# Experts ranked by load, with 64-token and 128-token experts in turn, in a mixture-of-experts stage

## The chip, the core and the metric

The kernel runs on one core of a Trainium2 chip. The core has TensorE (PE in the profile; its weight loads are PEld), VectorE (DVE), ScalarE (ACT), GpSimd (POOL) and SyncE (SP), which here only issues transfers, and 16 DMA engines. Each engine runs its own program in order; they wait for each other through semaphores. The metric is the device time of one execution in microseconds (us).

## What is computed

One layer of a diffusion backbone over 256 latent tokens of width 1024 (256 context tokens feed the first half of the layer). The first half is a token mixer (input projection, spatial gating, a gated delta rule, output projection). The second half is a mixture of experts, and that is where the change lies: 16 experts, of which each token takes 2, both from one group of four.

```python
def routed_moe(h, w_router, b_router, w1, w3, w2):
    scores = jax.nn.sigmoid(h @ w_router)
    sel = scores + b_router
    grp_score = jnp.sum(lax.top_k(sel.reshape(-1, N_GROUPS, EXPERTS_PER_GROUP), TOP_K)[0], axis=-1)
    best = jnp.argmax(grp_score, axis=-1)
    in_group = (jnp.arange(N_EXPERTS)[None, :] // EXPERTS_PER_GROUP) == best[:, None]
    _, idx = lax.top_k(jnp.where(in_group, sel, -jnp.inf), TOP_K)
    wts = jnp.take_along_axis(scores, idx, axis=-1)
    wts = wts / jnp.sum(wts, axis=-1, keepdims=True)
    ...
    for e in range(N_EXPERTS):
        y_e = (jax.nn.silu(h @ w1[e]) * (h @ w3[e])) @ w2[e]
        y = y + combine[:, e:e + 1] * y_e
    return y
```

`w1` and `w3` are 1024x512 and `w2` is 512x1024 for each expert, in float32: 6 MB an expert, 100.7 MB in all. 256 tokens x 2 choices are 512 rows of work, 32 an expert on average.

## The kernel before

All is written out by hand, with an order of its own for each engine. The expert stage begins at about 636 us.

**Routing and gather.** VectorE works out the two choices of each token (`chosen`); TensorE counts them, so that `counted` has each expert's number of rows and the first of them, and each of the 512 rows has a place in a list sorted by expert. TensorE gathers the tokens into that order by multiplying with a selection matrix (`pick`). ScalarE and VectorE copy the result to `hT`, split in a high part and a rest: every matmul of the stage is done as hi*hi, hi*lo and lo*hi in the type fp32r. `gather_copy` and `gather_low` are those copies; `h2_lo` is the rest of the tokens.

**An expert.** For each expert, in the order 0 to 15, GpSimd copies a window of 128 columns of `hT` that begins at the expert's first row (`take_window`; expert 0 reads `hT` itself). TensorE multiplies it with `w1` and `w3` (`up_half`, m = 0 and 1; 24 matmuls of 512 columns each), ScalarE takes the silu, VectorE the product (`act_product`), TensorE transposes it (`turn_act`, 4 transposes), ScalarE and VectorE split it (`act_high`, `act_low`), and TensorE multiplies with `w2` (`down_half`, twice 12 matmuls). ScalarE copies the result to `y_out` (`y_copy`) and GpSimd stores it with an indirect DMA, which skips the rows of the window that are not the expert's; the numbers for that come from `store_rows`. The last expert is stored by SP, all 128 rows, behind the 512 others (`LISTED` to `FIRST_TURN`). `place_rows`, on VectorE behind expert 1, works out where each token finds its two rows in the end. An expert of over 128 rows would go through `expert_turn`, which does not run here.

**The weights.** `STREAM` is the order of the 96 units of weights, 128x2048 floats (1 MB) each: the four up units of expert q, then the two down units of expert q-1. SP loads unit n into slot n % 5 (`SLOTS_AHEAD`) when unit n-5 is split. ScalarE casts a unit to `e_hi` (`expert_high`) and VectorE subtracts that from it to `e_lo` (`expert_low`); there are four buffers of each, so that the splits run up to four units ahead of TensorE. The semaphores are `landed`, `hi_ready`, `unit_split` and, for a unit that TensorE is through with, `unit_used`. In the profile the units are `raw`, and `e_hi` and `e_lo` are `w_hi` and `w_lo`.

**The constants.** GpSimd builds masks and counting rows (`order_mask`, `slot_iota`, `slot_row`) at the start of the program. It takes no part in the program between the last scan and the sum of squares `x_stat`.

## Time and profile before

| | us |
|---|---|
| three runs | 932.27, 930.23, 938.56; median 932.27 |
| the profiled execution, its own time | 937.08 |
| its span | 935.4 |
| PE busy | 818.2 (87%) |
| DVE busy | 625.3 (67%) |
| ACT busy | 516.1 (55%) |
| POOL busy | 224.9 (24%) |
| TensorE clock granted, mean | 0.963 |

The span is the time from the first to the last instruction of the profiled execution; its own time has in addition what lies around the instructions. The busy shares are means over stages of different kinds: up to 636 us the mixer, the routing and the gather, then the experts up to about 913 us, then the sum over each token's two rows and the output. In the rows further down, x12 is a count, "idle before" is the time an engine stood still ahead of an instruction, and the arrow names what ended it. The granted clock is 1.00 for 2.4 GHz and 0.50 for 1.2 GHz. A matmul's duration in a row includes its latency; matmuls overlap, so the distance between two starts tells the pace.

### The profile page before, as it was taken

The numbers are of one execution on the slowest core, as the hardware profiler recorded it, in microseconds if no ns is written. First come the engines' busy times: TensorE is split into PE (matmuls) and PEld (weight loads), VectorE is DVE, ScalarE is ACT, GpSimd is POOL, SyncE is SP. The second block draws the span as 40 slices with busy tenths as digits, with TensorE's granted clock in tenths as the row PEclk, the third lists the DMA queues.
The fourth block names the chain that finished last, engine by engine and source line by source line (L and its number), as shares of the span: only waits on it lengthen the run. The fifth ranks groups of instructions, "written<-read, shape, count | busy, mean of one in ns | idle before, by whom it ended". The sixth has DMA issues, their size and how long they took to land. (4 is left out here: it accounts for less than half of the span.)

```text
span 935.4 us, 15876 instructions
## 1 busy us (share of the span) xinstructions
PE 818.2 (87%) x6374; PEld 694.7 (74%) x6374; DVE 625.3 (67%) x804; ACT 516.1 (55%) x814; POOL 224.9 (24%) x336
## 2 busy tenths in 40 slices
PE   4998987999789997798769789949999999999990
PEld 2677875899669885698749788737888888888870
DVE  1596765458643585545455447678998998999965
ACT  3575742457414564236542344467777787777751
POOL 3114061124301243112410110016222322321112
PEclk9999999999989999999889999959999999999995
DMA  9977468345862358536687348807999999999944
GB/s 311 283 241 190 123 162 211 80 108 147 175 187 78 105 152 161 174 80 227 174 211 207 91 158 263 307 18 265 342 364 385 383 380 384 388 371 374 380 144 156
DMA packets 220052, 209.00 MB, mean 223 GB/s; under 512 B 51100, under 2 KB 156229, under 8 KB 219337
## 3 DMA queue, kind: packets, MB, share of 16 engines
q1 hardware_dynamic: 217241, 203.80, 69.5%
q0 software_dynamic: 2736, 4.15, 1.4%
q8 instruction: 52, 0.85, 0.4%
q14 instruction: 23, 0.19, 0.1%
HBM read 190.64 MB, written 23.10 MB: 229 GB/s over the span
## 5 line engine op out<-in xcount | busy, mean ns | idle before, releaser
L2061 DVE TENSOR_TENSOR w_lo<-raw,w_hi 128x2048 fp32r<-128x2048 f32 x96 | 233.3, 2450 | 24.3 <-ACT w_hi L1496 23.2
L2282 PE MATMUL bank<-hT,half_hi 128*128 128x256 f32 (+1 forms) x1024 | 231.1, 321 | 12.1 <-DVE half_lo L1616 5.9
L1496 ACT CAST w_hi<-raw 128x2048 fp32r<-128x2048 f32 x96 | 183.2, 1912 | 41.1 <-PE bank L2282 38.5
L2282 PEld LDWEIGHTS bank<-hT,half_hi 128*128 128x128 f32 x1024 | 169.5, 195 | 28.6 <-issue 8.0
L2282 PE MATMUL bank<-hT,half_lo 128*128 128x256 f32 (+1 forms) x512 | 160.8, 314 | 0.0
L2282 PE MATMUL bank<-w_hi,window 128*128 128x512 f32 x480 | 156.7, 397 | 0.0
L1616 DVE TENSOR_TENSOR half_lo<-half_raw,half_hi 128x1024 fp32r<-128x1024 f32 x88 | 108.8, 1237 | 55.9 <-ACT half_hi L1056 55.4
L2282 PE MATMUL bank<-lane 64*64 64x64 f32 (+2 forms) x2096 | 100.2, 233 | 21.7 <-issue 10.6
L2282 PEld LDWEIGHTS bank<-lane 64*64 64x64 f32 (+2 forms) x2096 | 91.5, 145 | 32.1 <-issue 17.4
L1056 ACT CAST half_hi<-half_raw 128x1024 fp32r<-128x1024 f32 x88 | 92.2, 1049 | 25.1 <-DMA half_raw<-in_w_out_dram 6.7
L2282 PEld LDWEIGHTS bank<-w_hi,window 128*128 128x128 f32 x480 | 90.3, 188 | 20.5
L2282 PEld LDWEIGHTS bank<-hT,half_lo 128*128 128x128 f32 x512 | 99.3, 194 | 5.5
L2282 PE MATMUL bank<-w_lo,window 128*128 128x512 f32 x240 | 94.7, 394 | 0.0
L1712 DVE SCALAR_TENSOR_TENSOR chan<-bank,conv_col,chan 128x508 f32<-128x508 f32 (+3 forms) x96 | 63.2, 658 | 8.1 <-ACT chan L1125 5.5
L967 POOL CAST window<-hT 128x2048 fp32r x15 | 39.7, 2652 | 113.7 <-PE bank L2282 90.0
L882 POOL TENSOR_TENSOR lane<-v_nat,gates 128x256 f32<-128x256 f32 x32 | 25.1, 788 | 142.1 <-DVE lane L1796 120.3
L2282 PEld LDWEIGHTS bank<-w_lo,window 128*128 128x128 f32 x240 | 45.2, 188 | 10.0
L2282 PE MATMUL bank<-w_hi,act_hi 128*128 128x512 f32 x128 | 50.6, 395 | 1.5 <-DVE act_lo L2214 1.5
L997 POOL DMA_INDIRECT expert_rows<-y_out,store_int x15 | 26.7, 1782 | 99.7 <-ACT y_out L1534 99.7
L2282 PE MATMUL bank<-w_hi,act_lo 128*128 128x512 f32 x128 | 50.5, 395 | 0.0
L2282 PE MATMUL bank<-w_lo,act_hi 128*128 128x512 f32 x128 | 50.4, 394 | 0.0
L1133 ACT ACTIVATE tanh_buf<-chan 128x512 f32<-128x512 f32 (+1 forms) x24 | 13.4, 559 | 40.3 <-DVE chan L1712 40.2
(321 smaller groups left out, 1269.2 us busy)
## 6 DMA issues: line engine op xcount, KB each, us to landing
raw<-in_w_e_dram SPq DMA_DIRECT2D x96, 1024.0 KB, 8.8
half_raw<-in_w_in_dram SPq DMA_DIRECT2D x64, 512.0 KB, 5.0
half_raw<-in_w_ada_dram SPq DMA_DIRECT2D x32, 512.0 KB, 4.8
raw<-in_w_ada_dram SPq DMA_DIRECT2D x8, 1024.0 KB, 11.4
dense<-staged SPq DMA_DIRECT2D x32, 128.0 KB, 4.5
half_raw<-in_w_proj_a_dram SPq DMA_DIRECT2D x8, 512.0 KB, 5.3
half_raw<-in_w_proj_b_dram SPq DMA_DIRECT2D x8, 512.0 KB, 4.1
half_raw<-in_w_out_dram SPq DMA_DIRECT2D x8, 512.0 KB, 8.3
```

The source lines that it names most:

```text
L882: last = pool.tensor_tensor(v_beta[pos % 2][:, :, d, :], v_nat[i % 2][:, :, t, :], gates[:, BETA, t, 2 * i:2 * i + 2, d:d + 1].to_broadcas ...
L967: pool.tensor_copy(window[q % 2][:, :, :, :], hT[:, :, :, bass.ds(at, P)].bitcast(F32)) .then_inc(s["window_ready"], 1)
L997: pool.indirect_dma_start(out=y_dram[0:LISTED, :], out_offset=to, in_=y_out[q % 2][:, :], in_offset=None, bounds_check=LISTED - 1, oob_is_ ...
L1056: act.copy(half_hi[m % HBUF][:, :], half_raw[n % HRING][:, :]).then_inc(s["half_high"], 1)
L1133: act.activation(tanh_buf[n % 2][:, 0:w], chan[n % 3][:, 0:w], ACT.Tanh, scale=0.5)\
L1496: act.copy(e_hi[n % WBUF][:, :], slots[n % SLOTS_AHEAD][:, :]).then_inc(s["hi_ready"], 1)
L1616: dve.tensor_tensor(half_lo[m % HBUF][:, :], half_raw[n % HRING][:, :], half_hi[m % HBUF][:, :].bitcast(F32), ALU.subtract).then_inc(s["ha ...
L1712: ins = dve.scalar_tensor_tensor(out=y[:, :, a:b], in0=ps[:, :, a + o:b + o], scalar=conv_col[:, CONV_KIND[n // 2], 2 * j + n % 2, tap:tap ...
L2061: dve.tensor_tensor(e_lo[n % WBUF][:, :], slots[n % SLOTS_AHEAD][:, :], e_hi[n % WBUF][:, :].bitcast(F32), ALU.subtract)\
L2282: return nc.tensor.matmul(dst, lhsT, rhs, start=start, stop=stop)
```

## The change

Experts 0 and 1 stay as they are. The other 14 are ranked by their number of rows when the counts are there, and the stream takes them in an order of ranks, wide and narrow in turn: places 2, 4, 6, 8, 10, 12 and 15 are narrow, 64 tokens, and hold the seven least loaded experts; places 3, 5, 7, 9, 11, 13 and 14 are wide, 128 tokens, and hold the seven most loaded. The eighth most loaded of 512 rows has at most 64. A number (`rank_at`) says which rank stands at which place.

A narrow expert's weights are not split. TensorE reads the f32 unit from its slot, in two column halves of the array: 64 output rows are one half of the columns of a unit, the other 64 the other half. So the expert takes 32 f32 matmuls of 256 columns up, 2 transposes and 8 of 512 down, in place of 48, 4 and 24. ScalarE and VectorE cast and split 54 units in place of 96. The slot of a narrow unit comes free with `unit_used`, not with `unit_split`. The two down units of a narrow expert are waited for together and used in alternation, so both are released by its last matmuls. The window of a narrow expert is the sum of both parts of `hT`, 64 columns. Its result is 128x512 and its store has half the bytes a row.

SP reads the number of the next expert from `order_int` and forms the addresses of the weights from it. VectorE ranks (`rank_loads`) ahead of the first copy of the gather, and orders counts and firsts (`order_experts`) behind the third split. `place_rows` has three operations more, since the last expert in the stream is now any of 14. The constants of GpSimd are built later, and there are more of them.

```diff
-FIRST_TURN = LISTED + 128
+FIRST_TURN = LISTED + 64
...
+WIDE, NARROW = P, P // 2
+FIXED = 2
+RANKED = EXPERTS - FIXED
+WIDTH = [WIDE, WIDE] + 6 * [NARROW, WIDE] + [WIDE, NARROW]
...
+        SPLIT_UNITS = [n for n, (_, q, _) in enumerate(STREAM) if WIDTH[q] == WIDE]
...
+            expert = list(range(FIXED))
             for n, (v, q, half_) in enumerate(STREAM):
-                if n >= SLOTS_AHEAD:
-                    sp.wait_ge(s["unit_split"], n - SLOTS_AHEAD + 1)
...
+                if n == UP_FIRST[FIXED]:
+                    sp.wait_ge(s["routing_ready"], 2)
+                if q == len(expert):
+                    expert.append(sp.value_load(order_int[0:1, q:q + 1], min_val=FIXED, max_val=EXPERTS - 1))
+                before = n - SLOTS_AHEAD
+                if before >= 0 and before in SPLIT_UNITS:
+                    sp.wait_ge(s["unit_split"], SPLIT_UNITS.index(before) + 1)
+                elif before >= 0:
+                    sp.wait_ge(s["unit_used"], before + 1)
...
+            sp.wait_ge(s["y_copied"], 2 * EXPERTS)
             for nh in range(2):
-                sp.wait_ge(s["y_copied"], 2 * (EXPERTS - 1) + nh + 1)
-                sp.dma_start(y_dram[last_rows, nh * N:nh * N + N], y_out[1][:, nh * N:nh * N + N]).then_inc(s["stored"], 16)
+                sp.dma_start(y_dram[LISTED:FIRST_TURN, nh * N:nh * N + N], y_out[1][NARROW * nh:NARROW * nh + NARROW, 0:N])\
+                    .then_inc(s["stored"], 16)
...
+                    pool.tensor_tensor(narrow_window[q % 2][:, :, :], hT[:, 0, :, bass.ds(at, NARROW)].bitcast(F32),
+                                       hT[:, 1, :, bass.ds(at, NARROW)].bitcast(F32), ALU.add).then_inc(s["window_ready"], 1)
...
+            def rank_loads():
+                key, at_rank = load_rank[:, 0, :], load_rank[:, 1, :]
+                square_of = [P, RANKED, RANKED]
+                dve.wait_ge(s["h2_split"], 2)
+                own.after(dve.scalar_tensor_tensor(out=key, in0=counted[:, 0, FIXED:], scalar=float(EXPERTS),
+                                                   in1=slot_iota[:, 0:RANKED], op0=ALU.mult, op1=ALU.subtract))
+                own.after(dve.tensor_tensor(holder[:, :, :], key.unsqueeze(1).to_broadcast(square_of),
+                                            key.unsqueeze(2).to_broadcast(square_of), ALU.is_ge))
+                own.after(dve.tensor_reduce(at_rank, holder[:, :, :], AX, ALU.add))
+                own.after(dve.tensor_tensor(holder[:, :, :], at_rank.unsqueeze(1).to_broadcast(square_of),
+                                            rank_at[:, :].unsqueeze(2).to_broadcast(square_of), ALU.is_equal))
+                own.after(dve.tensor_tensor(ranking[:, 0, :, :], holder[:, :, :],
+                                            slot_iota[:, FIXED - 1:EXPERTS - 1].unsqueeze(1).to_broadcast(square_of), ALU.mult))
+                own.after(dve.tensor_reduce(load_rank[:, 0, :], ranking[:, 0, :, :], AX, ALU.add))
+                dve.tensor_copy(order_int[:, FIXED:], load_rank[:, 0, :]).then_inc(s["routing_ready"], 1)
...
             expert_low(1)
+            rank_loads()
             gather_low(0)
             expert_low(2)
             gather_low(3)
             gather_low(6)
             expert_low(3)
+            order_experts()
...
+            def narrow_up(q, m):
+                dst = work_bank(q, m)
+                if m == 0:
+                    pe.wait_ge(s["window_ready"], q)
+                    pe.wait_ge(s["act_split"], q - 1)
+                for kh in range(2):
+                    weights = unit_landed(UP_FIRST[q] + 2 * m + kh)
+                    for kc in range(4):
+                        c = 4 * kh + kc
+                        for half in range(2):
+                            ins = mm(dst[NARROW * half:NARROW * half + NARROW, 0:256], narrow_window[q % 2][:, c, :],
+                                     weights[:, kc, 256 * half:256 * half + 256], c == 0, c == KC - 1)
+                    ins.then_inc(s["unit_used"], 1)
...
+            def narrow_down(q):
+                pe.wait_ge(s["act_split"], q + 1)
+                pe.wait_ge(s["y_copied"], 2 * (q - 2) + 2)
+                weights = [unit_landed(DOWN_FIRST[q] + nh) for nh in range(2)]
+                for c in range(4):
+                    half = c // 2
+                    for nh in range(2):
+                        ins = mm(work_bank(q, 2)[NARROW * nh:NARROW * nh + NARROW, :],
+                                 act_narrow[:, c % 2, NARROW * half:NARROW * half + NARROW], weights[nh][:, c, :], c == 0, c == 3)
+                        if c == 3:
+                            ins.then_inc(s["unit_used"], 1)
```

TensorE, in the middle of the stage. Before, from the transposes of one expert into the second half of the next one's up, as all experts have it (arena_hi is the product, window the expert's tokens, w_hi and w_lo the split weights):

```order
L2285 MATMUL bank<-ident,arena_hi 128x128 x4
L2282 MATMUL bank<-w_hi_49,window_65 128x512
L2282 MATMUL bank<-w_lo_50,window_65 128x512
L2282 MATMUL bank<-w_hi_49,window_65 128x512 x2
L2282 MATMUL bank<-w_lo_50,window_65 128x512
L2282 MATMUL bank<-w_hi_49,window_65 128x512 x2
```

Now, from the down projection of a narrow expert over the up of the next narrow one to the down of the wide one between them:

```order
L2414 MATMUL bank<-w_hi,window_68 128x512
L2414 MATMUL bank<-raw,act_narrow 64x512 x8
L2414 MATMUL bank<-raw,narrow_window_69 64x256 x8
L2414 MATMUL bank<-raw_78,narrow_window_69 64x256 x8
L2417 MATMUL bank<-ident,arena_hi 128x128 x4
L2414 MATMUL bank<-raw,narrow_window_69 64x256 x16
L2414 MATMUL bank<-w_hi,act_hi 128x512
L2414 MATMUL bank<-w_lo,act_hi 128x512
```

Behind 24 wide up matmuls there now stand six narrow units in a row, two down and four up, straight from the slots (`raw`, `raw_78`), and the wide down comes last.

VectorE, from the rest of the gathered tokens (h_lo) to the first experts' splits (w_lo). Before:

```order
L2162 TENSOR_TENSOR h_lo<-arena_hi,h_hi 128x1024 x2
L2061 TENSOR_TENSOR w_lo<-raw,w_hi 128x2048
L2158 CAST hT<-bank 128x512
L2061 TENSOR_TENSOR w_lo<-raw,w_hi 128x2048
L2158 CAST hT<-bank 128x512 x2
L2061 TENSOR_TENSOR w_lo_67<-raw,w_hi 128x2048
L2061 TENSOR_TENSOR w_lo_50<-raw_68,w_hi_49 128x2048
```

Now:

```order
L2147 TENSOR_TENSOR w_lo<-raw,w_hi 128x2048
L2253 SCALAR_TENSOR_TENSOR load_rank<-counted,slot_iota 128x14
L2255 TENSOR_TENSOR holder<-load_rank 128x196
L2257 TENSOR_REDUCE load_rank<-holder 128x14
L2258 TENSOR_TENSOR holder<-load_rank,rank_at 128x196
L2260 TENSOR_TENSOR ranking<-holder,slot_iota 128x196
L2262 TENSOR_REDUCE load_rank<-ranking 128x14
L2263 CAST order_int<-load_rank 128x14
L2244 CAST hT<-bank 128x512
L2147 TENSOR_TENSOR w_lo<-raw,w_hi 128x2048
L2244 CAST hT<-bank 128x512 x2
L2147 TENSOR_TENSOR w_lo_77<-raw,w_hi 128x2048
```

Seven operations stand between the second split and the first copy of the gather; seven more (order_experts) follow behind the last row shown.

SP, in the stream of the weights, with what each issue waits for. Before, all along the stage:

```order
L555 DMA raw<-in_w_e_dram 128x4x512 [waits unit_split] x4
L555 DMA raw_68<-in_w_e_dram 128x4x512 [waits unit_split]
L555 DMA raw<-in_w_e_dram 128x4x512 [waits unit_split] x4
L555 DMA raw_68<-in_w_e_dram 128x4x512 [waits unit_split]
L555 DMA raw<-in_w_e_dram 128x4x512 [waits unit_split] x4
```

Now, over some units of a narrow and the next wide expert (TENSOR_LOAD reads the expert's number; ISA forms an address):

```order
L586 DMA raw<-in_w_e_dram 128x4x512
L586 ISA [waits unit_used]
L586 DMA raw_78<-in_w_e_dram 128x4x512
L586 DMA raw<-in_w_e_dram 128x4x512 [waits unit_used]
L586 DMA raw<-in_w_e_dram 128x4x512 [waits unit_split]
L586 ISA [waits unit_split]
L586 DMA raw<-in_w_e_dram 128x4x512
L586 ISA [waits unit_split]
L586 DMA raw<-in_w_e_dram 128x4x512
L821 TENSOR_LOAD order_int
L821 ISA x2
```

Half of the issues now wait for `unit_used`, that is for TensorE, and no longer for the split.

## Rows read from the trace of the kernel before

**Rows 1.** Windows: PE, PEld, DVE, ACT, POOL busy; clock; DMA share; GB/s.

```profile
595.00:600.00 5.00, 5.00 (x27) 4.16 (x27) 3.40 (x5) 2.62 (x5) 0.00 (x0) 1.00 1.05 392
700.00:720.00 20.00, 20.00 (x90) 16.24 (x89) 18.69 (x10) 15.82 (x13) 4.95 (x3) 1.00 1.05 384
```

**Rows 2.** Tile view of raw (the weight units), 660 to 890 us.

```profile
L2061 DVE TENSOR_TENSOR w_lo<-raw,w_hi x81: 2278/2293/3417, 658.4 to 887.2; 128x2048 fp32r<-128x2048 f32 x81
L1496 ACT CAST w_hi<-raw x81: 1905/1912/1921, 659.3 to 888.1; 128x2048 fp32r<-128x2048 f32 x81
...
  PE bank L2282: 32.5, 52
...
  DMA raw<-in_w_e_dram: 2.7, 3
...
DMA to landing us min/median/max: 6.8/8.9/10.1
```

**Rows 3.** The same view, the one unit issued from 631 to 632 us.

```profile
DMA to landing us min/median/max: 5.1/5.1/5.1
```

**Rows 4.** Timeline of GpSimd: stores of experts 2, 4 and 12.

```profile
702.38 1.88 POOL L997 DMA_INDIRECT expert_rows<-y_out,store_int  x1 [5.57 <-ACT y_out L1534]
...
736.72 1.89 POOL L997 DMA_INDIRECT expert_rows<-y_out,store_int  x1 [5.57 <-ACT y_out L1534]
...
874.10 1.90 POOL L997 DMA_INDIRECT expert_rows<-y_out,store_int  x1 [5.56 <-ACT y_out L1534]
```

**Rows 5.** Timeline: first matmul of a down projection, VectorE's act_lo, next expert's up.

```profile
710.51 0.39 PE L2282 MATMUL bank<-w_hi,act_hi 128*128 128x512 f32 x1
716.08 0.39 PE L2282 MATMUL bank<-w_hi,window 128*128 128x512 f32 x1
...
706.12 0.68 DVE L2214 TENSOR_TENSOR act_lo<-bank,act_hi 128x512 fp32r<-128x512 f32 x1
```

**Rows 6.** Timeline of TensorE: f32 matmuls on four column tiles of 32.

```profile
473.53 1.92 PE L2282 MATMUL bank<-half_raw,cond_pad 128*32 128x512 f32 x16 [0.46 <-ACT staged L1179]
```

**Rows 7.** Windows (columns as rows 1) and timeline of TensorE around two gaps.

```profile
450.00:454.00 4.00, 3.07 (x14) 3.07 (x15) 1.23 (x1) 3.26 (x8) 1.47 (x3) 0.50 0.45 66
454.00:458.00 4.00, 4.00 (x31) 4.00 (x30) 0.94 (x2) 1.81 (x2) 1.73 (x7) 0.79 0.60 164
...
625.00:630.00 5.00, 3.03 (x8) 2.44 (x9) 4.96 (x7) 1.27 (x3) 0.00 (x0) 0.52 0.01 3
...
450.93 0.79 PE L2282 MATMUL bank<-hT,half_hi 128*128 128x256 f32 x2 [3.99 <-ACT staged L1179]
...
626.97 5.22 PE L2282 MATMUL bank<-pick,h_hi 128*128 128x512 f32 x16 [4.92 <-DVE pick L2150]
```

**Rows 8.** Timeline of VectorE and TensorE from the routing to the first expert.

```profile
618.85 0.33 DVE L2114 TENSOR_TENSOR cmp_a<-contest 128x160 f32<-128x160 f32 x1
...
632.68 0.69 DVE L2158 CAST hT<-bank 128x512 fp32r<-128x512 f32 x1 [1.32 <-PE bank L2282]
...
641.35 5.59 DVE L2061 TENSOR_TENSOR w_lo<-raw,w_hi 128x2048 fp32r<-128x2048 f32 x2 [2.39 <-ACT w_hi L1496]
...
636.32 0.47 PE L2282 MATMUL bank<-w_hi,hT 128*128 128x512 f32 x1 [0.50 <-DVE hT L2158]
```

**Rows 9.** Timeline from the last expert to the final sum.

```profile
906.59 0.96 POOL L997 DMA_INDIRECT expert_rows<-y_out,store_int  x1 [13.45 <-ACT y_out L1534]
...
910.76 3.14 SPq L798 DMA_DIRECT2D expert_rows<-y_out  x2
...
917.60 2.48 DVE L2262 SCALAR_TENSOR_TENSOR y_tok<-y_tok,pair_weight,ada_vec 128x1024 f32<-128x1024 f32 x2 [10.59 <-DMA y_tok<-expert_rows,row_int]
...
923.27 1.28 DVE L2262 SCALAR_TENSOR_TENSOR y_tok<-y_tok,pair_weight,ada_vec 128x1024 f32<-128x1024 f32 x1 [0.87 <-DMA y_tok<-expert_rows,row_int]
```

**Rows 10.** GpSimd's first instruction behind the scans, and VectorE's splits before 600 us.

```profile
609.93 0.54 POOL L955 TENSOR_TENSOR x_stat<-x_part 128x1 f32<-128x1 f32 x1 [52.60 <-ACT lane L1473]
...
L1616 DVE TENSOR_TENSOR half_lo<-half_raw,half_hi 128x1024 fp32r<-128x1024 f32 x88 | 108.8, 1237 | 55.9 <-ACT half_hi L1056 55.4
```

More of the change, by code:

```diff
@@ L539, in four, with wide_ahead @@
             return t[:, :].rearrange("p (c n) -> p c n", c=4)
+        SPLIT_UNITS = [n for n, (_, q, _) in enumerate(STREAM) if WIDTH[q] == WIDE]
+        SPLIT_TOTAL = len(SPLIT_UNITS)
+        WIDE_BEFORE = [WIDTH[:q].count(WIDE) for q in range(EXPERTS + 1)]
+        LAST_NARROW = TOP * SEQ - NARROW
+        def wide_ahead(q):
+            first = UP_FIRST[q] + WBUF
+            down = [n for n in (first, first + 1) if q and n in SPLIT_UNITS]
+            up = [n for n in range(UP_FIRST[q + 1] if q + 1 < EXPERTS else len(STREAM), len(STREAM))[:4] if n in SPLIT_UNITS]
+            return down, up
         def chunk_at(pos, d):
@@ L953, in _ @@
+            own.after(pool.tensor_tensor(slot_row[NARROW:P, 0, :], slot_row[NARROW:P, 0, :], narrow[NARROW:P], ALU.subtract))
+            own.after(pool.tensor_scalar(narrow[NARROW:P], narrow[NARROW:P], (P - 1.0) / NARROW, None, ALU.mult))
+            own.after(pool.tensor_tensor(slot_row[NARROW:P, 2, :], slot_row[NARROW:P, 2, :], narrow[NARROW:P], ALU.subtract))
             for t in range(2):
```

259 lines of the change are left out of this document (179 added, 80 removed).

## Prediction

> **What bounds the kernel now.** I read the windows of the expert stage first, because they show every engine, the transfers and the clock side by side. TensorE is busy all of each 20 us at the full clock, VectorE nearly, and the DMA share is 1.05 at 384 GB/s [rows 1]. Two things look full, and the question of this change is which one really is. With a deep queue of weights before the gather, the DMA engines show the same share of 1.05 and 392 GB/s [rows 1], so in the stage they are at their ceiling too. A unit of 1.05 MB at 390 GB/s takes 2.70 us.
>
> The tile view of the weights says the same from the other side. ScalarE's casts wait for TensorE 52 times and for a landing 3 times, but a unit takes 8.9 us from issue to landing [rows 2], against 5.1 us for one issued into an empty queue [rows 3]. Three units stand in the queue all the time. So TensorE sets the pace and the transfers are less than 2% from setting it: two experts take 736.72 - 702.38 = 34.34 us [rows 4], twelve units need 12 x 2.70 = 32.4 us, and two stores of results lie between them.
>
> **TensorE, narrow against wide.** Of 24 matmuls of a wide expert, 710.51 to 716.08 gives 0.232 us each, so a wide unit of 12 is 2.79 us [rows 5]. A narrow expert multiplies unsplit f32, 64 tokens wide, in two column halves of the array. No row has that shape. The nearest is w_ada: 8 matmuls of the program (16 in the trace) on four column tiles, 512 columns of f32, take 1.92 us [rows 6], so a round of tiles is 0.88 us, and it is short only if tiles run side by side. A narrow down projection is four rounds, 3.5 us; its 16 up rounds have half the columns, 0.44 us, 7.0 us, so 1.76 us a unit. Without overlap each doubles. Narrow: 10.5 us and turns, wide: 17.1. Added up, seven narrow experts save 7 x 6.4 = 45 us of TensorE. I don't take that: [rows 1, 2] say that transfers stop nearly all of it.
>
> **A loop that is new.** A slot of a wide unit comes free when it is split, up to four units ahead of TensorE. A slot of a narrow unit comes free when TensorE has used it, and both down units of a narrow expert are released together, at its end. From there one turn of the loop (two experts) is: the unit in flight and the two now issued land, 3 x 2.70 = 8.1 us (from an empty queue 5.1 + 2.7 = 7.8 [rows 3]); the third is a wide one, so it is cast, 1.91, and split, 2.29 [rows 2], with act_lo, 0.68 [rows 5], behind it on VectorE, and hand-overs, together 5.1; six wide units and their transposes, 17.1; the narrow down with its wait, 3.6. Sum 33.9 us, against 34.34: the loop keeps 0.4 us of the 6.4 that TensorE saves in it. TensorE stands idle in every turn: from the release it has four narrow up units and a turn, 7.4 us, and the first wide unit is ready after 13.2, so it waits 5.8 us.
>
> **What that gap does to the clock.** After a gap of 3.99 us ahead of 450.93 the granted clock is 0.50 up to 454 and 0.79 on average from 454 to 458: 4.75 us at the lower level of 1.2 GHz. After the gap ahead of 626.97 (4.92 us) it is 0.52 in 625 to 630, so 2.8 us of work at that level [rows 7]. The mean, 3.8 us, costs half of it, 1.9 us, because the matmuls behind a gap are wide ones. Bounds: nothing if the clock holds, 3.4 us if it stays low for 6.8. The Trainium skill ("TensorE: Matmul & The Clock Gate", section "Why this matters for your kernels") says to keep idle gaps out from between bursts of matmuls, because the clock drops behind them. It speaks against this change; the trace agrees, with the two gaps above.
>
> **The sum, on the profiled execution (span 935.4, own time 937.1).**
> - Head: seven VectorE operations that rank the loads stand ahead of the first gather copy. The nearest rows are 0.33 us for 128x160; five near 0.38 and two near 0.18, with hand-overs, make 2.5. VectorE was idle 1.32 us there, and TensorE waited 0.50 us for its copy [rows 8]: +1.2. The seven of order_experts (about 2.2) lie in VectorE's wait of 2.39 us just behind [rows 8]: 0, at most +1. Three operations more in place_rows: 0.5 us on VectorE, whose splits are ahead there: 0.
> - Expert 2 narrow: 4 x (2.79 - 1.76) = -4.1, its down -2.0, and unit 14, whose slot waits for unit 9, comes 1.3 late: -4.8. With the head -3.6.
> - Five turns of the loop (experts 3 to 12): 5 x (-0.4) = -2.0, clock 5 x 1.9 = +9.5: +7.5.
> - From there to TensorE's end it was 42.1 us: expert 12's store at 874.10 [rows 4] is some 3.3 us behind its down (a cast of 1.91 and a copy lie between), and the last copy's DMA is issued at 910.76 + 3.14 less its own 0.4, so TensorE ends at 912.9 [rows 9]. After: up 14 and turn 11.7, wait for late slots 1.7, down 13 5.6, up 15 and turn 7.4, wait for unit 92's split 4.0, down 14 5.6, clock 1.9, wait and down 15 4.2: 42.1, so 0.
> - Tail: VectorE starts on the first rows 11.0 us after expert 14's store (906.59 to 917.60) and works 4.8 us; the second rows begin at 923.27, 10.4 us after TensorE's end [rows 9]. A narrow last expert is so short that expert 14's store comes 3.8 us ahead of the end: VectorE is done at end + 12.0: +1.6.
> - GpSimd's constants move from the start into its wait of 52.6 us. Some 40 small operations, each held up at most by one VectorE split of 1.24 us, are 50 us [rows 10]: 0, and over that cover at most +2. SP reads each number ahead of a wait for a slot that it has anyway: 0. The list is written about 634, and unit 10's slot comes with unit 5's split, behind 641.35 [rows 8]: 0.
>
> Sum: -3.6 + 7.5 + 0 + 1.6 = +5.5 us, 0.6%. The three runs shown have a median of 932.27, 5 us under the profiled one; 932.3 + 5.5 = 938.
>
> **Rivals.**
> - *The halves do not run side by side.* A narrow unit is then 3.5 us, a narrow expert 21.5 instead of 17.1: 7 x 4.4 = +31, 963 us. For it: no row has 64 columns by 128 rows in f32. Against: four tiles overlap in [rows 6]. On the full array 16.24 us of weight loads lie beside 20 us of matmuls [rows 1], so loads do not push them apart. (The Trainium skill, "TensorE: Matmul & The Clock Gate", "Part 3: Packing small matmuls", has loads overlap running matmuls only in another row group; by that rule narrow experts would come near this rival, and the trace disagrees with it.) Chance 0.09.
> - *The clock stays low longer*, or the loop's bubble grows with a store in it (a store already costs the queue about 1 us): 3.4 instead of 1.9 in six gaps, +9, and +3: 950. Chance 0.20.
> - *Faster: the transfers never run dry.* If a landing is due before the loop needs it, the stage ends by bandwidth alone. Transfers ended near 898 (issue 889.6 plus 8.4), TensorE 15 us later. Behind a narrow last unit it needs 4.5 instead: -10, tail +1.6, smaller stores up to -2: 922 to 924, without gaps and so without a low clock. It decides when the two down slots are released some 3 us sooner than I have them. Against: both wait for the last round, and five slots are all. Chance 0.12.
> - *TensorE's saving counts in full*: 932 - 45 = 887. It needs over 450 GB/s, and [rows 1] have 392. Chance 0.03.
> - *Forecast*, with hand-overs and clock losses between the bounds: 926 to 947. Chance 0.56.
>
> **The numbers.** 938 us is the forecast's. 924 to 950 takes in most of the second and third rivals and leaves out the first and the fourth. A measurement of this kernel can tell about 1%, 9 us, from no change. Over 1% faster: the fourth rival and most of the third, 0.12. Over 1% slower: the first two and the forecast's upper edge, 0.32. Within: 0.56.
>
> **What would show it.** Windows of the stage: TensorE at some 85%, clock below 1.00 once in each 34 to 36 us, DMA share near 1.0. The wait for the first wide unit behind four narrow ones should be 5 to 6 us, with VectorE's split or act_lo as releaser. Narrow up matmuls should come every 0.11 us (0.22 each, two at a time); 0.22 apart is the first rival. Stores of alternate experts should stand 34 to 37 us apart. The sum is wrong if those waits are absent, if weights move over 400 GB/s, or if the work ahead of 628 us has moved.

## The result, and the profile after

| | before | after |
|---|---|---|
| median, us | 935.25 | 951.86 (947.75 to 954.95) |
| ratio (95% interval) | | 1.0156 (1.0111 to 1.0201) |
| profiled execution: own time, span | 937.08, 935.4 | 953.67, 952.1 |
| PE, DVE, ACT busy, us | 818.2, 625.3, 516.1 | 792.8, 521.9, 429.5 |
| TensorE clock, mean | 0.963 | 0.945 |

The change makes the kernel 1.6% slower; repeated later (e0_after) it was 1.3% (949.55, ratio 1.0133, interval 1.0085 to 1.0181). TensorE is busy 25 us less, VectorE 103 us, ScalarE 87 us, and the end comes 12 to 17 us later.

The windows of the stage, with the columns of [rows 1]; the four short ones stand around the gap of the first turn:

```profile
700.00:800.00 100.00, 82.14 (x434) 57.05 (x431) 45.81 (x28) 42.44 (x35) 15.12 (x11) 0.90 0.99 363
800.00:900.00 100.00, 85.00 (x419) 59.03 (x418) 45.97 (x30) 42.15 (x34) 17.69 (x11) 0.93 0.94 344
...
700.00:708.50 8.50, 8.50 (x72) 4.83 (x68) 0.00 (x0) 0.58 (x1) 0.99 (x1) 1.00 0.98 336
708.60:714.40 5.80, 0.00 (x0) 0.00 (x0) 2.87 (x2) 3.26 (x3) 1.28 (x1) 0.92 1.05 391
714.50:720.30 5.80, 5.80 (x14) 4.54 (x15) 4.75 (x3) 4.46 (x4) 0.00 (x0) 0.50 1.04 387
720.40:736.00 15.60, 15.60 (x71) 11.63 (x72) 8.06 (x6) 5.84 (x6) 2.97 (x2) 1.00 1.04 391
```

Where [rows 1] had TensorE full at clock 1.00, it now works 82 to 85% of the time at 0.90 to 0.93. After a standstill of 5.8 us it works 5.8 us at half the clock.

What ended TensorE's waits in the stage (us in total, times, longest):

```profile
PE bank L2414 <- DVE act_lo L2342: 34.9, 7, 6.9
```

GpSimd's timeline, the stores of the narrow experts 2 and 10:

```profile
702.22 0.99 POOL L1070 DMA_INDIRECT expert_rows<-y_out,store_int  x1 [2.47 <-ACT y_out L1617]
...
848.77 0.98 POOL L1070 DMA_INDIRECT expert_rows<-y_out,store_int  x1 [2.47 <-ACT y_out L1617]
```

A turn of two experts takes (848.77 - 702.22) / 4 = 36.6 us, where it was 34.34 [rows 4]. Nearly all waits end with act_lo, as forecast.

One turn in the timelines of the engines (start, us, engine, line, operation; in brackets the idle time before and what ended it):

```profile
699.69 1.03 PE L2414 MATMUL bank<-raw,act_narrow 128*64 128x512 f32 x4
700.55 3.62 PE L2414 MATMUL bank<-raw,narrow_window 128*64 128x256 f32 x32
...
704.69 3.88 PE L2414 MATMUL bank<-raw,narrow_window 128*64 128x256 f32 x32
...
714.47 0.79 PE L2414 MATMUL bank<-w_hi,act_hi 128*128 128x512 f32 x1 [5.90 <-DVE act_lo L2342]
...
700.75 8.30 SPq L586 DMA_DIRECT2D raw<-in_w_e_dram  x6
...
709.60 1.90 ACT L1570 CAST w_hi<-raw 128x2048 fp32r<-128x2048 f32 x1 [8.17 <-DMA raw<-in_w_e_dram]
...
711.53 2.29 DVE L2147 TENSOR_TENSOR w_lo<-raw,w_hi 128x2048 fp32r<-128x2048 f32 x1 [13.66 <-ACT w_hi L1570]
713.74 0.68 DVE L2342 TENSOR_TENSOR act_lo<-bank,act_hi 128x512 fp32r<-128x512 f32 x1
```

This is the loop of the prediction, link by link. The narrow down projection ends at 700.7, SP issues at 700.75, ScalarE gets its unit at 709.6 after 8.17 us of waiting, cast and split end at 713.8, act_lo ends at 714.4, TensorE starts at 714.47. In ScalarE's waits from 660 to 890 us, which had 2.7 us and 3 times there in [rows 2], this now stands first:

```profile
ACT w_hi L1570 <- DMA raw<-in_w_e_dram: 68.0, 39, 8.9
```

### The profile page after: what moved, and what is told of

It reads as the page before. It is cut to its first block and busy times, and to the rows that moved or that the text cites. A ratio compares the mean times of both kernels' runs of the same rounds, so it can differ in the third digit from the quotient of the medians.

```text
span 952.1 us, 16050 instructions
## 1 busy us (share of the span) xinstructions
PE 792.8 (83%) x6416; PEld 648.3 (68%) x6416; DVE 521.9 (55%) x778; ACT 429.5 (45%) x758; POOL 208.4 (22%) x367
## 5 line engine op out<-in xcount | busy, mean ns | idle before, releaser
L2147 DVE TENSOR_TENSOR w_lo<-raw,w_hi 128x2048 fp32r<-128x2048 f32 x54 | 124.2, 2304 | 109.9 <-ACT w_hi L1570 109.8
L1570 ACT CAST w_hi<-raw 128x2048 fp32r<-128x2048 f32 x54 | 102.5, 1904 | 84.6 <-DMA raw<-in_w_e_dram 79.4
L2414 PE MATMUL bank<-w_hi,window 128*128 128x512 f32 x256 | 83.7, 398 | 1.0 <-DVE w_lo L2147 1.0
L2414 PEld LDWEIGHTS bank<-w_hi,window 128*128 128x128 f32 x256 | 48.1, 188 | 13.3 <-DVE w_lo L2147 1.5
L915 POOL TENSOR_TENSOR lane<-v_nat,gates 128x256 f32<-128x256 f32 x32 | 24.9, 784 | 142.3 <-DVE lane L1881 119.0
L2414 PE MATMUL bank<-raw,narrow_window 128*64 128x256 f32 x448 | 51.7, 382 | 0.0
L2414 PE MATMUL bank<-w_lo,window 128*128 128x512 f32 x128 | 50.2, 392 | 0.0
L2414 PEld LDWEIGHTS bank<-w_hi,act_hi 128*128 128x128 f32 x72 | 16.8, 233 | 43.9 <-DVE act_lo L2342 38.0
L2414 PEld LDWEIGHTS bank<-raw,narrow_window 128*64 128x64 f32 x448 | 31.0, 137 | 19.8 <-issue 4.8
L2414 PE MATMUL bank<-w_lo,act_hi 128*128 128x512 f32 x72 | 32.9, 457 | 0.0
L2414 PE MATMUL bank<-w_hi,act_lo 128*128 128x512 f32 x72 | 32.7, 454 | 0.0
```

What stands on the lines that cost most here:

```text
L915: last = pool.tensor_tensor(v_beta[pos % 2][:, :, d, :], v_nat[i % 2][:, :, t, :], gates[:, BETA, t, 2 * i:2 * i + 2, d:d + 1].to_broadcas ...
L1570: act.copy(e_hi[k % WBUF][:, :], slots[n % SLOTS_AHEAD][:, :]).then_inc(s["hi_ready"], 1)
L2147: dve.tensor_tensor(e_lo[k % WBUF][:, :], slots[n % SLOTS_AHEAD][:, :], e_hi[k % WBUF][:, :].bitcast(F32), ALU.subtract)\
L2414: return nc.tensor.matmul(dst, lhsT, rhs, start=start, stop=stop)
```

## The experiments

Three stretches of the profiled execution, from its timelines: "gather" is when its first matmul starts, "stage" goes from there to TensorE's end, "rest" to the end of the span; they add up to the span, to 0.1 us.

| kernel | median, ratio to before, interval | gather | stage | rest |
|---|---|---|---|---|
| before | 935.25 to 938.33 | 626.97 | 285.9 | 22.5 |
| after | 951.86, 1.0156 (1.0111 to 1.0201) | 631.66 | 295.1 | 25.3 |
| e0_after | 949.55, 1.0133 (1.0085 to 1.0181) | 628.23 | 293.2 | 26.0 |
| e1_blocks | 938.70, 1.0003 (0.9975 to 1.0031) | 638.24 | 281.6 | 24.0 |
| e2_act_first | 948.68, 1.0105 (1.0056 to 1.0154) | 628.49 | 291.8 | 26.0 |
| e3_fill | 943.71, 1.0053 (1.0022 to 1.0085) | 630.99 | 286.9 | 25.8 |
| e4_consts_back | 949.43, 1.0102 (1.0055 to 1.0150) | 631.55 | 294.6 | 25.9 |
| e5_before_half | 937.77, 0.9984 (0.9952 to 1.0015) | 629.82 | 287.4 | 23.6 |
| e6_after_half | 924.65, 0.9854 (0.9801 to 0.9907) | 629.31 | 267.2 | 25.6 |
| e8_two_narrow | 937.60, 0.9985 (0.9962 to 1.0008) | 633.78 | 279.5 | 24.5 |
| e9_down_early | 941.68, 1.0024 (0.9994 to 1.0054) | 629.52 | 284.1 | 26.2 |
| e10_three_narrow | 934.73, 0.9971 (0.9942 to 1.0001) | 633.43 | 277.3 | 24.9 |
| e11_all_three | 937.22, 0.9978 (0.9952 to 1.0005) | 636.07 | 277.3 | 25.5 |
| e12_two_stores | 943.18, 1.0022 (0.9987 to 1.0056) | 631.64 | 288.6 | 22.5 |

**Is it the taking in turn?**

```diff
-WIDTH = [WIDE, WIDE] + 6 * [NARROW, WIDE] + [WIDE, NARROW]
+WIDTH = 9 * [WIDE] + 7 * [NARROW]
```

> The changed kernel with the places put differently: places 0 to 8 wide, 9 to 15 narrow, nothing in turn; the same seven narrow experts, the same work. My theory is that the loss comes from taking them in turn (one slot loop, one idle gap and one fall of the clock per narrow and wide pair), and that the gain has its ceiling in the transfers, 2.70 us a unit. Then seven wide experts cost 17.17 us each as before, seven narrow ones 6 x 2.70 = 16.2, and TensorE ends 4.5 us behind the last landing where it was 15: 7 x 0.97 + 10.5 = 17 us less, less some 4 for the head and the tail: 922 beside 935 for the kernel before (ratio 0.986), no idle time over 3 us in the stage. Against it stands that TensorE then works 10.5 of each 16.2 us: if the clock falls to the lower level through the narrow part, a narrow expert is up to 21 us long and the time 945 to 950. If TensorE's saving counted in full (second rival): 890. If taking them in turn is not what costs: 950 as the changed kernel.

Windows 700 to 800 us (wide) and 874 to 892 us (narrow):

```profile
700.00:800.00 100.00, 100.00 (x456) 80.92 (x457) 84.34 (x45) 71.32 (x56) 27.59 (x13) 1.00 1.03 382
...
874.00:892.00 18.00, 13.00 (x82) 6.83 (x82) 0.85 (x2) 0.97 (x2) 1.45 (x2) 0.91 1.04 375
```

TensorE's waits:

```profile
PE bank L2414 <- DMA raw<-in_w_e_dram: 24.6, 11, 4.2
```

GpSimd's stores of the narrow experts 10 and 14:

```profile
848.41 1.00 POOL L1070 DMA_INDIRECT expert_rows<-y_out,store_int  x1 [9.53 <-ACT y_out L1617]
...
916.81 0.97 POOL L1070 DMA_INDIRECT expert_rows<-y_out,store_int  x1 [16.09 <-ACT y_out L1617]
```

The same seven narrow experts in a row cost nothing against before (1.0003) and are 12 us cheaper than in turn (938.70 against 950.7, the mean of the two medians): the order of the places is what costs. But my 922 was wrong too. A narrow expert takes (916.81 - 848.41) / 4 = 17.1 us, not 16.2, although TensorE works only 13 of 18 us, and so is as long as a wide one, 17.17, to 0.1 us. The stores explain little of the 0.9: four narrow ones, from 836 to 904 us, moved 0.21 MB together, 0.05 each. The transfers were not full. The windows of one narrow expert, around the end of a down projection:

```profile
868.00:880.00 12.00, 7.75 (x44) 3.48 (x44) 0.79 (x2) 0.00 (x0) 1.25 (x1) 0.87 1.03 386
880.00:887.00 7.00, 7.00 (x56) 4.24 (x52) 0.43 (x1) 0.97 (x2) 0.99 (x1) 0.98 1.02 350
```

Behind the release of both down slots the rate is 350 GB/s where it was 386, which over 7 us is 0.65 us of transfers lost. I had left out that narrow slots are held until use here too. TensorE's waits now end mostly with landings. The low clock behind them (0.91) seems to cost nothing, since what follows waits for transfers too; no run isolates that.

**Who sets 17.17 us in the kernel before?** From unit 12 on, only half of every unit is transferred (`load(four(slot)[:, 0:2], src[:, 0:2], ...)`), in the kernel before and in the changed one.

> The kernel before, but from unit 12 on each transfer of weights brings only the first half of its unit (1024 of 2048 floats in each row); casts, splits and matmuls work on what lies in the slot, so the weights of the experts from 2 on are partly left out. It tells what TensorE and VectorE need when transfers are no bound. Theory: in the kernel before TensorE and the transfers are both full (17.1 us of matmuls, and 6 x 2.70 + 1 us for the store of results = 17.2 us of transfers an expert), so TensorE alone still sets 17.1: the time stays within 0.5% (930 to 937). Rival: transfers set the pace already and TensorE waits for them here and there: over 1% faster.

> The changed kernel with the same half transfers from unit 12 on (weights of the experts from place 2 on partly left out). Theory: the transfers and the loop through the slots hold TensorE back, so its saving shows as soon as they are short. The three landings in the loop shrink from 8.1 to some 4 us: a turn of 36.8 becomes 30 to 32.5 (TensorE's own sum is 17.1 + 10.5 = 27.6), the gap 1 to 3 us; five turns give 22 to 34 us, and the time is 918 to 930 beside 950. If the clock no longer falls because the gaps are short, 910. Rival: the loop of casts and splits holds it, not the transfers: 940 or more.

Window 700 to 800 us of e5_before_half:

```profile
700.00:800.00 100.00, 100.00 (x445) 81.15 (x444) 92.09 (x46) 78.29 (x59) 25.39 (x12) 1.00 0.64 199
```

The same window of e6_after_half, then its waits of TensorE:

```profile
700.00:800.00 100.00, 89.84 (x473) 62.58 (x471) 48.36 (x30) 42.10 (x36) 19.84 (x12) 0.93 0.64 201
```

```profile
PE bank L2415 <- DVE act_lo L2343: 15.1, 5, 4.9
```

With half the bytes the kernel before keeps its time, and from the first expert matmul to TensorE's end its 276.6 us to a tenth: TensorE alone needs 17.17 us an expert. (What the transfers need is in e12.) The changed kernel gains 25 us (two timed runs): only when transfers are cheap does TensorE's saving show. Its turn falls to 33.3 us, not to 30 to 32.5, and gaps of 2.4 to 4.9 us stay, still ended by act_lo. Half a unit doesn't land in half the time: from the end of the narrow down projection to the cast behind the gap's landing it was 5.2, 6.6, 5.7, 5.3 and 5.2 us in the five turns, mean 5.6, where the expectation had some 4 and the changed kernel 8.7 to 9.7, mean 9.0. That is 3.4 us less, and the turn became 3.3 us shorter (36.6 to 33.3).

**What does a store take from the transfers?** Each result of the experts 0 to 11 is stored a second time, into spare rows.

```diff
+                if q < 12:
+                    pool.indirect_dma_start(out=y_spare[0:LISTED, :], out_offset=to, in_=y_out[q % 2][:, :], ...
```

> The kernel before with the result of each of the experts 0 to 11 stored twice, the second time into rows that nobody reads. Nothing else. It measures what a store takes from the transfers of weights. Theory: a store takes some 0.97 us of the queue's time (34.34 us a pair less 12 x 2.70, halved), and the transfers are within 0.1 us of TensorE's pace, so an expert goes from 17.17 to about 18.1 us and the time up by 10 to 12 us (ratio 1.011 to 1.013). Rival: the queue has room and TensorE alone sets 17.17: up by less than 3 us.

GpSimd's first store of the experts 4 and 8:

```profile
742.05 1.89 POOL L998 DMA_INDIRECT expert_rows<-y_out,store_int  x1 [6.17 <-ACT y_out L1538]
...
815.42 1.89 POOL L998 DMA_INDIRECT expert_rows<-y_out,store_int  x1 [10.20 <-ACT y_out L1538]
```

Bytes that GpSimd's stores moved (packets, MB, share) from 742 to 815 us, which are the eight of experts 4 to 7, and from 815 to 866 us, the six of experts 8 to 10:

```profile
q0 software_dynamic: 1152, 2.62, 9.1%
...
q0 software_dynamic: 864, 0.62, 3.8%
```

When the transposes of the experts 8 and 9 start on TensorE, and a window:

```profile
795.09 0.60 PE L2289 MATMUL bank<-ident,arena_hi 128*128 128x128 f32 x4
813.28 0.60 PE L2289 MATMUL bank<-ident,arena_hi 128*128 128x128 f32 x4
```

```profile
800.00:820.00 20.00, 19.41 (x83) 14.59 (x82) 17.68 (x11) 14.89 (x12) 8.72 (x4) 1.00 1.04 384
```

ScalarE's waits from 660 to 890 us:

```profile
ACT w_hi L1500 <- DMA raw<-in_w_e_dram: 37.0, 52, 2.7
```

Both sides were half right. ScalarE, which follows the landings, takes (815.42 - 742.05) / 4 = 18.3 us an expert in this stretch, and waits for landings 52 times instead of 3 [rows 2]. 18.34 less 16.2 is two stores: 1.07 us each. But these are four heavily loaded experts: 2.62 MB in eight stores is 0.33 MB or 80 rows each, where 32 rows are the average, and 0.33 MB at 390 GB/s would be 0.84 us. Experts 8 to 10 have 0.62 / 6 = 0.10 MB or 25 rows a store, and there, with both stores still made, ScalarE takes (866.43 - 815.42) / 3 = 17.0 us an expert, so at most 0.4 us a store. A store's price goes with its rows. With one store the transfers need 16.2 + 1.07 = 17.3 us at experts 4 to 7, as much as TensorE, and 16.6 us at experts 8 to 10, 3% less.

The stage is only 2.7 us longer (the timed ratio, 1.0022, can't be told from no change), because transfers, casts and splits run ahead of TensorE. TensorE kept 17.17 us an expert up to 795.09, and only then took 18.2 (813.28 - 795.09) and 18.4 (831.69 - 813.28), at the pace of the transfers. Counted from the first expert's matmul (636.32 in the kernel before, 641.05 here), ScalarE is 5.7 us late at the store of expert 10 (850.14 against 839.75) and TensorE 2.4 us at the transposes of expert 11, at the same time (849.03 against 841.88): the lead that was used up is some 3 us.

**The clock.** 22 matmuls that nobody reads stand in each of the five gaps:

```diff
+                if 4 <= q <= 12 and WIDTH[q] == NARROW:
+                    for c in range(FILL):
+                        mm(work_bank(q, 3)[:, :], hT[:, 0, 0, 0:P], hT[:, 0, 1, :], True, True)
                 if q:
                     down_of(q - 1)
```

> The changed kernel, and 22 matmuls of 128x512 that nobody reads fill the gap in front of the wide expert's down projection at the narrow places 4 to 12 (22 x 0.232 = 5.1 of some 5.9 to 6.1 us), into a bank that is free there. The rest is the same. Clock theory: 4.9 us of work at the lower clock behind each of five gaps is what they cost besides standing still, so with the gaps filled the clock stays at the full level and 5 x 2.4 = 12 us come back: 940 beside 952. Rival: the time behind the gap is bound by transfers, so that a faster TensorE only waits longer at the next gap: the filled gaps grow by what the clock gives and the time is that of the changed kernel, 0 to -2 us.

Timeline of TensorE in the first filled gap:

```profile
708.89 5.28 PE L2415 MATMUL bank<-hT 128*128 128x512 f32 x22
714.90 0.50 PE L2415 MATMUL bank<-w_hi,act_hi 128*128 128x512 f32 x1 [0.73 <-DVE act_lo L2343]
```

Window of the whole stage:

```profile
640.00:906.00 266.00, 252.57 (x1333) 179.29 (x1331) 140.55 (x116) 120.69 (x101) 59.31 (x41) 1.00 0.99 357
```

The clock is 1.00 from 640 to 906 us, and work that is thrown away makes the kernel 6 us faster than e0_after and e4_consts_back (943.7 against 949.5). The first gap ends at 714.90, no sooner against the gather than without filling, so it is the clock that pays. The rival (0 to -2 us) falls. But 1.6 us a turn came back (34.97 us by its stores at 702.77 and 842.66), not 2.4: part of what the clock gives is lost at waits for landings and splits, since a turn nears the transfers' own length.

**The loop.** Two edits that shorten it. First the split of the activation ahead of the first down unit's cast and split:

```diff
-                for n in down[:1]:
-                    expert_low(n)
                 if q and WIDTH[q - 1] == WIDE:
                     act_low(q - 1)
+                for n in down[:1]:
+                    expert_low(n)
```

(at the narrow places, and the same with `expert_high` and `act_high`.)

> The changed kernel, and at the narrow places the split of the wide expert's activation (act_hi on ScalarE, act_lo on VectorE) stands ahead of the cast and split of the first down unit, not behind it. My theory has act_lo as the last link of the loop in front of TensorE's gap, 0.68 us and a hand-over: each of five gaps ends 0.7 to 1.0 us sooner and each turn is as much shorter, 3.5 to 5 us in all (ratio to the changed kernel about 0.996), and the wait is then released by a split, VectorE's w_lo. Rival: the transfers alone pace the turn (a landing is late anyway): gap and turn stay, 0 us.

TensorE's waits, then the first matmul behind the first gap:

```profile
PE bank L2422 <- DVE w_lo L2150: 32.4, 11, 6.5
```

```profile
710.87 0.76 PE L2422 MATMUL bank<-w_hi,act_hi 128*128 128x512 f32 x1 [5.40 <-DVE w_lo L2150]
```

The releaser changed as expected and the gap is 0.5 us shorter, and the stage is 1.4 to 3.3 us shorter than in the three profiles without the edit (after, e0, e4). In the time (948.68 against 949.43 to 951.86) it can't be told from nothing; that it "helped alone", as the expectation of e11_all_three says, is not shown. Then the narrow down projection ahead of the wide expert's fourth up unit, so that its two slots come free one wide unit sooner:

```diff
                 for kh in range(2):
+                    if q and WIDTH[q - 1] == NARROW and m == 1 and kh == 1:
+                        narrow_down(q - 1)
                     n = UP_FIRST[q] + 2 * m + kh
```

> The changed kernel, and where a narrow expert stands ahead of a wide one its down projection comes ahead of the wide one's fourth up unit, not behind it (counts of the semaphore adapted). Its two slots come free 2.8 us sooner. Theory of the loop from release to release (landings, cast and split, six wide units, narrow down): it loses one wide unit, 36.8 becomes 34.0 to 35, near the 34.3 that transfers and stores need, so the gap falls from some 6 to 3 or 4 us and five turns give 9 to 14 us: 938 to 942 beside 950. If the two down units have not landed by then (they landed only 1.4 to 4 us ahead of their use), half of that. Rival: the release of the slots is not in the loop: no change.

TensorE's waits, then its timeline at the first gap, which was 5.90 us:

```profile
PE bank L2421 <- DVE act_lo L2349: 21.3, 6, 4.9
PE bank L2421 <- DVE w_lo L2154: 4.1, 7, 1.4
PE bank L2421 <- DMA raw<-in_w_e_dram: 3.7, 3, 1.7
```

```profile
694.24 3.65 PE L2421 MATMUL bank<-raw,act_narrow 128*64 128x512 f32 x16 [1.68 <-DMA raw<-in_w_e_dram]
...
713.52 0.53 PE L2421 MATMUL bank<-w_hi,act_hi 128*128 128x512 f32 x1 [4.85 <-DVE act_lo L2349]
```

8 us came back (941.68 against 949.55), by a change of place alone: the release of the slots is in the loop. It is less than 9 to 14, and the case that the expectation named is there: down units had not landed when TensorE now wanted them (3.7 us of waiting in three places, 1.68 here).

**Do the three add up?** Narrow and wide still in turn:

> The changed kernel (narrow and wide in turn) with all three edits that helped alone: activation split first, narrow down projection earlier, and 12 matmuls that nobody reads in the gap. A turn (two experts) was 36.7 us, and alone they brought it to 36.3, 35.2 and 35.0. If they add up, a turn is 33.1 and the time 934 to 935 (ratio 0.997). Theory of the ceiling: twelve units of 2.70 and two stores need 34.3, as in the kernel before, so a turn is 34.3 to 34.7 and the time 938 to 940 (ratio 1.000 to 1.003); TensorE's waits are then for landings (DMA), in several short pieces.

GpSimd's stores of the experts 2 and 10:

```profile
709.16 0.99 POOL L1078 DMA_INDIRECT expert_rows<-y_out,store_int  x1 [0.16 <-issue]
...
844.73 0.99 POOL L1078 DMA_INDIRECT expert_rows<-y_out,store_int  x1 [0.16 <-issue]
```

The window 700 to 780 us, the landings of weights from 700 to 850 us, and TensorE's waits:

```profile
700.00:780.00 80.00, 76.72 (x430) 51.19 (x428) 33.97 (x22) 30.02 (x26) 15.05 (x10) 1.00 1.05 387
```

```profile
DMA to landing us min/median/max: 7.1/9.2/11.5
```

```profile
PE bank L2430 <- DVE w_lo L2158: 12.0, 8, 2.1
```

A turn is 135.57 / 4 = 33.9 us, between 33.1 (all add up) and 34.3 (the ceiling as I had it). The DMA share is 1.05 at 387 GB/s from 700 to 780 us, which is as full as [rows 1] show it, and no unit lands in under 7.1 us, where one from an empty queue took 5.1 [rows 3]. The first two turns, which lie there, took 33.0 and 33.8 us (stores at 709.16, 742.19 and 775.96). So the transfers allow some 33 to 34 us, and my ceiling of 34.3 was too high. TensorE then waits in many short pieces for splits, that is for landings behind them, rather than for DMA directly. The gap to the kernel before is closed (0.9978), and no more.

**What narrow experts can bring at all.** Two at the end; and three, one of them at place 2, with both edits of the loop:

```diff
+WIDTH = 14 * [WIDE] + 2 * [NARROW]
```

```diff
+WIDTH = [WIDE, WIDE, NARROW] + 11 * [WIDE] + 2 * [NARROW]
```

> The changed kernel with only two narrow experts, at the last two places (14 wide, 2 narrow); ranking and all else stay. Where TensorE and the transfers are both full (17.2 us an expert), a narrow expert can only pay where the transfers have ended: in the kernel before TensorE ends 15 us behind the last landing. Theory: no loop of narrow and wide, so the stage is that of the kernel before up to expert 13; the end comes 5 to 6 us sooner (after 13 and ahead of 14 all five slots stand full until TensorE takes them, so not all 10 us of the lag); the ranking costs 0.9 and the last store is 1 to 2 us later against TensorE's end: 934 to 936 beside 938 (ratio 0.995 to 0.998). Rival: the stall at the first narrow expert eats all of it: 938 to 940, as in the kernel with seven narrow experts at the end (ratio 1.000).

> As the run with two narrow experts at the last places, and place 2 narrow as well, with two edits that shortened the loop: the split of the wide activation first, and the narrow down projection ahead of the wide expert's fourth up unit. In the changed kernel place 2 brought 3.9 us up to its own end, and the one gap behind it costs some 2 of them again: 932 to 934 beside 938 (ratio 0.993 to 0.996). Rival: from place 3 on the pace is that of full transfers, and what was won at place 2 is lost as waits of TensorE right behind: as with two narrow experts.

TensorE's timeline at the end of e10_three_narrow:

```profile
907.04 3.65 PE L2429 MATMUL bank<-raw,act_narrow 128*64 128x512 f32 x16 [1.39 <-DMA raw<-in_w_e_dram]
```

The last two narrow down projections wait for landings (1.42 us at 901.63, and this one), so TensorE now ends right behind the transfers. The stages are 6.4 and 8.6 us shorter than before's and the rest 2.0 and 2.4 us longer. By that the whole should be 4.4 and 6.2 us shorter; the timed runs give 1.4 (0.9985) and 2.7 (0.9971), and neither interval excludes no change. So e10_three_narrow is the fastest of all whole kernels here, and it isn't shown to beat the kernel before.

**The part ahead of the gather.** The block of constants, from `order_mask` to the last operation on `slot_row`, back at the start of GpSimd's program; and the changed kernel itself once more:

> The changed kernel with GpSimd's constants (order_mask, slot_iota, slot_row and the new ones) built at the start of the program again, where the kernel before has them. In the changed kernel's profile everything up to the gather is 4.7 us later than in that of before, and the moved constants are the only edit ahead of it. I take those 4.7 us for a difference between two executions, not for a price of the move: the time then is that of the changed kernel within 0.3%, and its gather begins anywhere between 627 and 632. Rival: the move costs them (GpSimd work at the wrong place, or other transfers): 947 beside 952, gather at 627.

> The changed kernel itself once more, so that the other kernels are set against it on the same chip. 950 us and a ratio of 1.010 to 1.016 to the kernel before. If the 4.7 us that its first profile lost ahead of the gather are a difference between executions, its gather begins at another time here, anywhere from 627 to 638, as it did in the four other profiles of such kernels (628.5, 631.0, 631.5, 638.2).

The gather's first matmul, in the profile of e0_after:

```profile
628.23 6.39 PE L2414 MATMUL bank<-pick,h_hi 128*128 128x512 f32 x16 [4.92 <-DVE pick L2236]
```

The unchanged kernel repeated starts it 3.4 us sooner than in its first profile, and the one with the constants back at 631.55, so the 4.7 us are mostly a difference between executions. (The gather starts at 632.0 us on average in the ten profiles that build the constants late, spread over 10 us, and at 630.0 in the four that build them early.) Whether the moved constants cost anything stays open. The ratios of e4 and e0 differ by 0.3% with 0.5% on either side. But take stage and rest of the table against before's 308.4 us, and set that beside the timed ratio: in the ten kernels that build the constants late the timed loss is 2 us more on average (3 to 4 in e1, e8, e10 and e11), in the three that build them early (e4, e5, e12) it is 2 us less. A price of up to some 4 us is not excluded, and no run here isolates it.

## Why the prediction was right or wrong

The direction of the forecast and its mechanism hold; its size doesn't. The measured 951.86 and 949.55 lie above the likeliest case (926 to 947 us) and at the second rival's 950, just over and just inside the range's edge, and the loss is over the 1% within which the forecast had put it (1.3 to 1.6% for 0.6%). Some 3 of the 14 us between 938 and 951.86 are the base: the forecast added to 932.27, and the same kernel's median was 935.25 beside the changed one. That the time is the second rival's is partly luck: it put 1.5 us a gap more on the clock and 3 us in all on the loop, and the runs show 0.5 us a gap and 0.8 us a turn. In the profiled execution +16.7 us stand against +5.5:

| step | forecast | after | 
|---|---|---|
| up to the gather's first matmul | 0 | +4.7 |
| rank_loads ahead of the first copy | +1.2 | +0.8 |
| expert 2 narrow, with unit 14 late | -4.8 | -3.9 |
| five turns of the loop | +7.5 | +12.4 |
| last part of the stage | 0 | -0.1 |
| from TensorE's end on | +1.6 | +2.8 |

- **What bounds it: nearly right in rate, incomplete.** That TensorE sets the pace held (half transfers change nothing), and so did that the transfers are less than 2% from setting it, for experts 4 to 7; for experts 8 to 10 it was 3% (e12_two_stores). But the argument counted rates only. The transfers also had a lead, of which e12_two_stores used up some 3 us, and as I read the gaps, the narrow experts throw it away, because their slots stay taken until TensorE is through (e9, where they come free sooner, speaks for that, and so does the lower rate behind each release in e1).
- **Narrow matmuls: right.** Halves run side by side. A narrow down projection took 3.65 us (forecast 3.5), the two halves of the up projection 3.62 and 3.88 (7.0 together). The first rival is out. (The Trainium skill, "TensorE: Matmul & The Clock Gate", "Part 3: Packing small matmuls", has weight loads overlap only in another row group; the trace disagrees again, with 3.65 us for eight matmuls of 512 columns that all use the same rows. The same section has column tiles run side by side, and there the trace agrees.)
- **The loop: mechanism and links right, one link too short.** From the release to the needed landing I had 8.1 us; it was 709.6 - 700.7 = 8.9 (8.7 to 9.7 in the five turns). The two slots are issued 0.57 us apart into a queue that has nearly run empty, the first unit lands after 5.8 us and the second 3.1 later, where the sum from an empty queue had 5.1 [rows 3] and 2.7. Cast, split, act_lo and hand-overs were 714.47 - 709.6 = 4.9 (5.1). The gaps were 5.9 to 6.9 us (forecast 5.8), and the first term that was too small is this one: 8.9 us for 8.1, +0.8 a turn.
- **The clock: right that it falls, too small.** Behind the first gap TensorE worked 5.8 us at the lower level (the window from 714.50 above), behind the other four 3.0, 4.6, 5.6 and 5.3:

```profile
751.40:754.40 3.00, 2.99 (x7) 2.42 (x8) 3.00 (x3) 1.92 (x2) 0.00 (x0) 0.50 1.04 387
787.40:792.00 4.60, 4.60 (x11) 3.63 (x12) 4.60 (x3) 3.25 (x2) 0.00 (x0) 0.50 1.04 386
823.90:829.50 5.60, 5.60 (x13) 4.43 (x14) 5.19 (x4) 3.81 (x3) 0.00 (x0) 0.50 1.05 389
861.80:867.10 5.30, 5.30 (x13) 4.15 (x14) 4.88 (x4) 3.80 (x3) 0.00 (x0) 0.50 1.05 387
```

  Mean 4.9, half of it lost: 2.4 us a turn, against 1.9 from two gaps of [rows 7] (4.75 and 2.8). Two samples, one of them low, had given the mean; 5.8 us is the longest such stretch, and no run shows the 6.8 us of the upper bound. +0.8, +0.5 and -0.2 (the hand-overs) explain the turn: the forecast had 33.9 + 1.9 = 35.8 us, and it was (884.8 - 700.7) / 5 = 36.8 from one narrow down projection's end to the sixth's. (The Trainium skill, "TensorE: Matmul & The Clock Gate", "Why this matters for your kernels", has the rule to keep idle gaps from between bursts of matmuls. It spoke against the change, and e3_fill agrees: filled gaps kept 1.00 and gave back 6 us.)
- **Expert 2: nearly right**, -3.9 for -4.8. rank_loads ran as costed (seven operations, 635.97 to 638.3), with 1.10 us of waiting by TensorE behind it for 0.50 before. But its +0.8 is no larger than the difference between executions: from the gather's first matmul to the first expert's it was 9.35 us before, 10.2 after, 10.5 in e0_after, where the wait is 0.49, and 10.8 in e5_before_half, which ranks nothing.
- **The tail: right in kind, 1.2 us too small.** The store of expert 14 came 3.0 us ahead of TensorE's end (923.83 and 926.8), not 3.8, and the sums began 11.35 us behind it, not 11.0:

```profile
923.83 0.96 POOL L1066 DMA_INDIRECT expert_rows<-y_out,store_int  x1 [16.75 <-ACT y_out L1611]
935.18 2.48 DVE L2394 SCALAR_TENSOR_TENSOR y_tok<-y_tok,pair_weight,ada_vec 128x1024 f32<-128x1024 f32 x2 [12.08 <-DMA y_tok<-expert_rows,row_int]
```

  The second rows are no longer waited for; the first rows, which need expert 14's store, set the end, as said.
- **The constants: right as far as seen.** They ran from 561.6 to 566.8 us, a tenth of the 50 us that I had bounded them with, and GpSimd still stood idle 49.03 us (52.60 in [rows 10]). What comes of the open point above would be the one thing missing here.
- **The third and fourth rivals** are out as they stood: bubbles in the transfers and gaps were there in every turn, and none of the windows above shows more than 392 GB/s. Yet the third had a point: freeing the down slots one wide unit (2.8 us) sooner was e9, and it gave back two thirds of the loss (7.9 of 11.4 us). I had looked at the last round of the narrow down, not at its place in the order.

## What to carry over

Where two resources are equally full, halving the work of one gains nothing until the other is relieved; ask for the lead between them too, since a change that gives it up (slots held until use, released in pairs) costs at once, at the length of a landing. A gap that comes back in each turn is paid twice here, as time and as clock, so first move the release of the buffer forward in the order of the program, which was worth 8 us here without removing any work. Put the cheap units where the other resource has finished: seven narrow experts at the end cost 12 us less than in turn, though no arrangement of narrow experts here is shown to beat the kernel before. And look at what a measured piece carries before you call its price typical: the stores of four loaded experts cost over twice as much as those of the next ones.

## What the runs showed of the hardware

- An indirect store of a result took 1.07 us of the transfers' time beside weights where it moved 0.33 MB (80 rows of 4 KB; 0.84 us at 390 GB/s), and at most 0.4 us where it moved 0.10 MB (25 rows, e12_two_stores).
- The clock did not follow the length of a gap alone. It fell after 5.9 to 6.9 us, after 3.6 to 4.2 us in e1_blocks, after 2.54 and 2.92 us in e6_after_half, after 2.74 us at 912.5 in the changed kernel and after 2.14 us in e11_all_three. It stayed at 1.00 after gaps of 1.3 to 1.4 us, after 2.76 us in e0_after (the same place that fell after 2.74), after 2.93 us in e8_two_narrow (901.2 to 904.2) and after 3.38 us in e1_blocks (820.8 to 824.2).
- Half a unit took 5.2 to 6.6 us from the release of its slots to the cast, a whole one 8.7 to 9.7 us (e6_after_half, the changed kernel).
- Matmuls that nobody reads made the kernel faster than standing still, by 6 us in 950.
